# Seven block products instead of eight for gate and up of twelve chunks of layer 0, with the 22 chunks in parts of 6, 8 and 8

## The reference, cut to what matters

```python
D_MODEL = 1024
D_FF = -(-8 * D_MODEL // (3 * 256)) * 256      # 2816

def _swiglu(h, w_gu, w_down):
    g, u = jnp.split(h @ w_gu, 2, axis=-1)
    return (jax.nn.silu(g) * u) @ w_down

for l in range(DEPTH):
    mods = jnp.split(c_act @ w_ada[l] + b_ada[l], 6, axis=-1)      # and the same of cc_act for the context
    ...
    f = _swiglu(_modulate(_layernorm(x), sh2, sc2), w_gu[l], w_down[l])
    x = _layernorm(DEEPNORM_ALPHA * x + g2 * f, ln2_g[l], ln2_b[l])
```

## Time and profile before

| what | value |
|---|---|
| median of 3 runs | 2298.59 us (2298.22 to 2300.33) |
| the profiled execution's own time | 2300.03 us |
| its span, first to last instruction | 2298.2 us |
| mean granted TensorE clock (1 is full speed) | 0.997 |
| busy: PE, DVE, ACT, POOL | 2245.5, 1206.5, 940.1, 1108.4 us |
| matmul instructions | 12986 |
| share of the chain that ended last: PE, DVE, ACT, POOL | 84%, 8%, 4%, 1% |

### The profile page before, as it was taken

How to read it: one execution, slowest core, us unless ns; L and a number is a source line. 1 busy time by engine, 2 the same in 40 slices (tenths; PEclk the granted TensorE clock), 3 DMA queues, 4 the chain that set the end, 5 groups by cost and what they waited for, 6 DMA issues and landing times.

```text
span 2298.2 us, 34335 instructions
## 1 busy us (share of the span) xinstructions
PE 2245.5 (98%) x12986; PEld 2054.7 (89%) x12986; DVE 1206.5 (52%) x2473; ACT 940.1 (41%) x1874; POOL 1108.4 (48%) x868
## 2 busy tenths in 40 slices
PE   7999999999999999999999999999999999999997
PEld 4899989989999999999998888888888899888887
DVE  6979766538731646654832364656637536112114
ACT  4232466437622751111112364256546547222223
POOL 1334455435534453433534563456545567545545
PEclk9999999999999999999999999999999999999999
DMA  6634300122224445443523453221223256333335
GB/s 270 218 116 133 102 19 28 57 79 82 60 65 149 154 161 183 135 154 111 167 88 118 152 170 123 69 60 38 65 87 97 83 193 189 119 96 101 110 117 186
DMA packets 122535, 270.27 MB, mean 118 GB/s; under 512 B 13972, under 2 KB 14228, under 8 KB 120984
## 3 DMA queue, kind: packets, MB, share of 16 engines
q1 hardware_dynamic: 112032, 242.28, 32.9%
q10 hardware_dynamic: 10360, 26.09, 3.5%
HBM read 254.68 MB, written 10.49 MB: 115 GB/s over the span
## 4 chain that ended last, share of the span: by engine, by line
PE 84%; DVE 8%; ACT 4%; POOL 1%; issue 1%; DMA 1%; ACTq 1%; SPq 0%; DVEq 0%
PE ps L2047 32%; PE ps L2059 13%; PE ps L2049 12%; PE ps L2476 7%; PE ps L2160 7%; PE ps L2429 3%; PE ps L2411 3%; PE ps L2392 2%; PE ps L2236 1%; POOL w_lo L610 1%; DVE pt L1741 1%; DVE max_c L1724 1%; DVE ada_unused_merge_c L1261 1%; DMA raw<-in_stream 1%; ACT p_sb L987 1%
## 5 line engine op out<-in xcount | busy, mean ns | idle before, releaser
L610 POOL TENSOR_TENSOR w_lo<-raw,w_hi 128x512 fp32r<-128x512 f32 x648 | 888.5, 1394 | 915.9 <-ACT w_hi L688 915.1
L688 ACT ACTIVATE w_hi<-raw 128x512 fp32r<-128x512 f32 x648 | 377.4, 627 | 663.7 <-PE ps L2049 215.1
L2047 PE MATMUL ps<-h_hi,w_lo 128*128 128x512 f32 (+1 forms) x832 | 304.7, 366 | 0.0
L2047 PE MATMUL ps<-h_hi,w_hi 128*128 128x512 f32 (+1 forms) x832 | 303.9, 365 | 0.0
L2047 PE MATMUL ps<-h_lo,w_hi 128*128 128x512 f32 (+1 forms) x832 | 303.9, 365 | 0.0
L622 POOL TENSOR_TENSOR p_sb<-p_sb,row_inv 128x768 f32<-128x768 f32 (+1 forms) x160 | 179.1, 1128 | 196.6 <-DVE row_inv L1734 195.2
L1851 DVE TENSOR_TENSOR ps<-silu_g,ps 128x512 f32<-128x512 f32 (+3 forms) x52 | 36.7, 706 | 355.1 <-PE ps L2047 191.1
L2047 PEld LDWEIGHTS ps<-h_hi,w_lo 128*128 128x128 f32 x832 | 156.2, 188 | 18.6 <-POOL w_lo L610 0.3
L2047 PEld LDWEIGHTS ps<-h_lo,w_hi 128*128 128x128 f32 x832 | 156.2, 188 | 18.4
L2047 PEld LDWEIGHTS ps<-h_hi,w_hi 128*128 128x128 f32 x832 | 156.2, 188 | 18.3
L2476 PE MATMUL ps<-h_hi,w_lo 128*128 128x384 f32 (+1 forms) x408 | 146.7, 360 | 1.0 <-ACT gates_a L1024 0.7
(11 more groups left out here) (248 smaller groups left out, 5345.1 us busy)
## 6 DMA issues: line engine op xcount, KB each, us to landing
raw<-in_stream SPq DMA_DIRECT2D x648, 256.0 KB, 3.0
ada_raw_gate_up<-in_w_ada SPq DMA_DIRECT2D x48, 512.0 KB, 3.5
ada_raw_tokens_a<-in_w_ada SPq DMA_DIRECT2D x16, 512.0 KB, 4.7
ada_raw_merge_c<-in_w_ada SPq DMA_DIRECT2D x16, 512.0 KB, 3.7
bias_sb<-in_bias ACTq DMA_DIRECT2D x32, 256.0 KB, 2.9
scratch<-xr ACTq DMA_DIRECT2D x16, 512.0 KB, 4.7
xr<-scratch SPq DMA_DIRECT2D x14, 512.0 KB, 5.0
first_raw<-in_w_first SPq DMA_DIRECT2D x5, 1024.0 KB, 14.4
```

The lines of the kernel that those rows point to most:

```text
L610: nc.gpsimd.tensor_tensor(w_lo[:, u % 2, cols], raw[:, u % 2, cols], w_hi[:, u % 2, cols].bitcast(F32), ALU.subtract).then_inc(S("lo_made" ...
L688: nc.scalar.activation(w_hi[:, s, cols], raw[:, s, cols], ACT.Copy).then_inc(S("hi_made"), 1)
L2047: last = nc.tensor.matmul(bank(0), tile, x[:, k, 0:split], start=start, stop=stop)
```

## The change

- Gate and up of layer 0's chunks in parts 1 and 2 that are 768 tokens wide (8 and 4 chunks) are made from seven block products per chunk instead of eight. A chunk's operands are a 2 x 2 block matrix of weights (gate and up, by the two halves of the 1024 input features; each block 128 by 512, a half unit) and one of activations (input halves by two halves of 384 tokens). The seven weight factors are three of the four blocks and four sums or differences of blocks, made by DVE (`first_sums_of`, `last_sum_of`). The activation factors are three blocks of `h` and four sums or differences (`crossed`), which are split once into `crossed_hi` and `crossed_lo`. Each product is 12 matmuls of 384 columns, so a chunk has 84 instead of 96.
- ACT makes seven high parts per chunk and POOL seven low parts, in four half slots of `w_hi`/`w_lo` (`factor_split`, `factor_lows`). DVE combines the products by five additions of 384 columns.
- Ten additions of 1536 columns build `crossed`, two behind each of the first five units of down of part 0 (`crossing`, `beside_down`). ACT makes their four high parts in one go behind its fifth unit (`crossed_his`), DVE the four rests after the sixth.
- The parts are 6, 8 and 8 chunks in both layers. Beside layer 0's chunks now stand 18 of the 48 `w_ada` units: four groups of three beside the two chunks that are left of part 0 after the lead, and two groups beside down of part 0. Units 66 to 96 move to layer 1: 15 beside `tokens_a`, 15 beside `merge_c`. From unit 64 on only the latent condition is multiplied.

```diff
-PARTS = ((0, 8), (8, 6), (14, 8))
+PARTS = ((0, 6), (6, 8), (14, 8))
...
-ADA_WINDOWS = {"tokens_a": (16, 32), "merge_c": (32, 48)}
-ADA_LOADS = {"tokens_a": {2: 3, 3: 3, 4: 3, 5: 3, 6: 3, 7: 1}, "merge_c": {3: 3, 7: 2, 8: 3, 9: 2, 10: 3, 11: 3}}
-ADA_AFTER_PAIR = (4, 6, 6, 0)
-
-ADA_BESIDE = {("gate_up", 0): (48, 4), ("down", 0): (60, 4), ("gate_up", 1): (72, 3), ("down", 1): (81, 4),
-              ("gate_up", 2): (93, 1)}
+ADA_WINDOWS = {("tokens_a", 0): (16, 32), ("merge_c", 0): (32, 48), ("tokens_a", 1): (66, 81), ("merge_c", 1): (81, 96)}
+ADA_LOADS = {("tokens_a", 0): {2: 3, 3: 3, 4: 3, 5: 3, 6: 3, 7: 1}, ("merge_c", 0): {3: 3, 7: 2, 8: 3, 9: 2, 10: 3, 11: 3},
+             ("tokens_a", 1): {2: 3, 3: 3, 4: 3, 5: 3, 6: 3}, ("merge_c", 1): {3: 3, 7: 2, 8: 3, 9: 2, 10: 3, 11: 2}}
+ADA_AFTER_PAIR = ((4, 6, 6, 0), (4, 6, 5, 0))
+ADA_BOTH = 64
+
+ADA_BESIDE = {("gate_up", 0): (48, 4), ("down", 0): (60, 2)}
...
             def beside(ph, u):
 
                 first, count = ada_beside(ph)
-                each = 4 if ph.kind == "gate_up" and ph.part else 2
-                n, rest = divmod(u - ph.unit - 2, each)
+                n, rest = divmod(u - ph.unit - 2, 1 if ph.kind == "gate_up" else 2)
...
             def down(ph):
+                nxt = after(ph)
+                if sevenfold(nxt):
+                    for n in range(KD):
+                        if n < KD - 2:
+                            unit_done(ph.unit + n, n % 2)
+                        else:
+                            act.wait_ge(S("unit_done"), ph.unit + n + 1)
+                            for j in range(2):
+                                factor_split(nxt, 2 * (n - KD + 2) + j)
+                        if n == KD - 4 and ph.part == 0:
+                            crossed_his(ph)
+                    return
...
+            def first_sums_of(ph, n):
...
+                nc.vector.tensor_tensor(factor_sum[:, :], u0, u1, ALU.add).then_inc(S("factor_summed"), 1)
...
+            def crossing(ph):
...
+                return [of(t1, hi[0, 1], hi[0, 0], ALU.subtract), of(t4, lo[0, 1], lo[0, 0], ALU.subtract), of(t1, t1, t4, ALU.add),
+                        of(t2, hi[1, 1], t1, ALU.subtract), of(t2, t2, lo[1, 1], ALU.add),
...
+                        if ada:
+                            for half in range(2):
+                                ada_three("gate_up", beside[0] // ADA_SLOTS + 2 * n + half)
...
+                def beside_down(n):
+
+                    for step in steps[2 * n:2 * n + 2]:
+                        step()
+                    if n == KD - 3 and steps:
+                        ada_biased(ADA_UNITS, ADA_BOTH, MODS_READY[1, 0])
+                        for x in range(4):
+                            crossed_rest(x)
+                    if n == KD - 2:
+                        first_sums_of(nxt, 0)
...
+                    for k in range(KD // 2):
+                        for name in TERMS:
+                            w, x = term(name, 0, x_hi, x_lo)
+                            last = nc.tensor.matmul(ps[:, bank, 0:HALF], half_slot(w, slot)[:, k * P:(k + 1) * P], x[:, first + k, a:a + HALF],
```

276 lines of the change are left out of this document (241 added, 35 removed).

## The result

The changed kernel takes **2323.9 us** (median of 4 runs, 2321.9 to 2327.3), against 2298.4 of the kernel before in the same session (4 runs, 2297.8 to 2300.3). The ratio is 1.0106, with a 95% interval of 1.0094 to 1.0119: 1.1% slower. The profiled execution has a span of 2321.6 us against 2298.2 and a mean granted clock of 0.988 against 0.997. The forecast was 2319, slower by over 0.2% with a chance of 0.65.

The account below looks back on a forecast made before the run. PE, busy 98% of the span, was taken as the bound: matmuls times spacing plus waits. -25.0 + 26.7 + 12.9 + 6.0 = +20.6 on 2298.6 gave 2319 us, range 2288 to 2330.

Parts of the forecast that it names:

- the three places: Where PE would wait: entry into the new loop (down of part 0), layer 1's `tokens_a` and its `merge_c`.
- Products, -25.0: Layer 0's 12 new chunks: each loses 12 matmuls of 0.1734 us, 25.0 us less.
- the loop at nothing: Loop of seven products: DVE and POOL fit in the 14.6 us of a chunk, so no added cost.
- R3: Rival: the new loop itself waits 1 us in each of 12 chunks, 2331 us; chance 0.07.
- R4: Rival: matmuls of the seven products are spaced wider than 173 ns, no gain, 2344 us; chance 0.03.
- Entry, 26.7: Part 0 into the new loop: DVE's late work delays down's last unit, 25.0 us, 26.7 with the clock.
- the predicted 963.4: Forecast start of down's last unit in part 0, against 938.5 undisturbed.
- DVE and POOL: In the entry: one waits for the other, a meeting costing DVE about 0.95 us, a POOL pair 1.9.
- `tokens_a`, 11.2 and 12.9 with the clock: Layer 1: fourth unit's weight load stands on SP behind `w_ada` loads waiting for DVE; 11.2 us, 12.9 with clock.
- `merge_c`, 5.2 and 6.0: Layer 1: ninth unit's weight load stands behind a held `w_ada` load; 5.2 us, 6.0 with part of a slow clock.
- The clock, 1.7 for a wait of 5 us or more: PE's granted clock falls after idling: 1.7 us lost, charged for each stall of 5 us or more.
- R1: Rival: DVE's slack covers the moved work, PE waits nowhere, 2274 us; chance 0.10.

Follow-up runs that it names:

- all_none: Changed kernel without loads and multiplications of layer 1's 48 `w_ada` units (48 to 95); 2276.7 us, 0.9902 of the kernel before.
- loads_alone: Changed kernel without DVE's multiplications of `w_ada` units 48 to 65, their loads, queue places and waits kept; 2300.1 us, 1.0005 of the kernel before.
- act_order: Changed kernel with ACT's four `crossed_hi` copies behind the split of down's last unit, not ahead of it; 2322.5 us, 1.0108 of the kernel before.
- loads_later: Changed kernel with only the steps moved at which SP issues layer 1's `w_ada` loads, same work; 2310.2 us, 1.0048 of the kernel before.
- spread_again: Changed kernel with ACT taking down part 0's sums, copies and factor sums reordered, entry units spread from the bridge, layer 1 loads re-placed; 2289.6 us, 0.9956 of the kernel before.

## Why the prediction was right

The direction and the three places are right, and the mechanism in each. The size of the entry is right partly by luck.

- *Products, -25.0, and the loop at nothing*: held. The spacing is 14.56 us a chunk; all_none gave back 22.5 of 25.0. R3 and R4 are out.
- *Entry, 26.7*: 27.6 measured (24.7 until the last unit of down starts, and 2.9 of clock behind it). That unit starts at 961.27. This execution comes to gate and up 1.9 us ahead of the one before (first silu at 868.06, 869.93 before), so the predicted 963.4 would be 961.5. The path there was split otherwise. The last hidden part was 2.7 us later than in my sum: eight of 24 multiplications took 2.1 to 2.3 us, and I had counted two pairs of meetings. Therefore the waits were 8.1, 4.3 and 7.5 and not 5.5, about 4 and "about 12". The tenth crossing ended at 953.4 (955.3 with the shift, foreseen 954.5). **This agreement is partly luck.** DVE began down 2.35 us later than in the sum (908.75, or 910.65 with the shift, against 908.3), and that should have come through to the last unit, since ACT's copies wait for DVE's whole stream. Two errors the other way hid it: DVE went from there to its tenth crossing in 44.6 us against 46.2, and from the crossing to the last unit it took 7.9 against 8.9, the four copies being 5.6 and not 6.2. That all but 1.8 us of the waits is DVE's multiplications is shown by loads_alone; that ACT's order is not needed for the loss, by act_order, and the prediction named it as if it were.
- *DVE and POOL*: the rows show 2.12 to 2.33 us for an instruction of 1.22, so 0.9 to 1.1 for a meeting; the rows' price of 0.95 held, the count of meetings did not. The Trainium skill, "SBUF — State Buffer", section "Who interferes with whom", calls the shared port pair an exclusive lock, by which I had allowed up to 1.28 us for each meeting, an estimate. This trace agrees that one waits for the other, and no meeting in the entry's 24 multiplications cost the full 1.28.
- *`tokens_a`, 11.2 and 12.9 with the clock*: 10.4 and 12.4. (The terms as written add to 1411.5 at most and 10.9, not to 1411.8 and 11.2.) The whole of it is SP's hold (loads_later). The Trainium skill, "DMA: Bandwidth & Descriptors", section "Anatomy of one DMA — SWDGE (gpsimd) path", says that a DMA's semaphore wait is spent on the issuing sequencer before dispatch. The loads here are issued by SP and not by GpSimd, and this trace agrees for them: the weight load issues at 1402.17, right behind the third held load.
- *`merge_c`, 5.2 and 6.0*: 7.7 (7.0 and a small one) and 10.3. **This term was too small.** The hold was foreseen (the weight load issues at 1501.2; I had 1488.9, and PE comes to this place 11.7 later than before, which makes 1500.6); the landing was not. I took 3.4 us, the median of the earlier trace rows; from issue to ACT's split it was 4.7, with five `w_ada` loads around it.
- *The clock, 1.7 for a wait of 5 us or more*: **the weakest step.** Five waits lost 12.0 us, 2.4 each. Of these the last three add to the sum's terms, 2.9, 2.0 and 2.6, together 7.5; I had charged 4.2 for them (the first wait's 1.7 lies inside the entry's 25.0). Taken from the earlier trace rows, 1.7 was the price of one stall at the start, of 4.3 us; the one of 4.26 us at 933.42 indeed lost 1.5, the four longer ones 2.0 to 3.05. The prediction took its price from the shortest stall and put it on all.

In sum, 20.6 predicted and 25.3 measured by these terms (25.5 by the medians); of the 4.7 us between them 3.3 are the clock and 2.5 `merge_c`'s wait, less 1.1 in the other two places.

R1 is what the repairs make of the change in part, and none reached 2274. The best, spread_again, still has four waits, of 1.3 to 5.4 us; that DVE's slack of some 2 us a unit is too small for all of the moved work fits this, but no run tests it by itself.
